# Top-k of the experts in four parts of two heads in place of two parts of four

## The chip, the cores and the metric

The program runs on 1 core of a Trainium2 chip. The metric is the device time of one execution in microseconds; before the change it was 2129.03 us, the median of 3 runs (2128.95 to 2151.08). Engines are PE (matrix), DVE (vector), ACT (scalar), POOL (GpSimd) and SP (which here only issues transfers); the core has 16 DMA engines.

## The reference

One layer on 512 prompt rows and 32 sample rows (8 sequences of 4). An attention block (compressed, selected and window keys) and a convolution are mixed and added to x; then each row looks up experts:

```
h2 = rms_norm(x, norm2) * (1 + sc2) + sh2
q  = (h2 @ peer_q).reshape(rows, 8 heads, 2, 128)
s  = einsum(q, peer_keys)                # 128 scores for each head and half
s1, i1 = top_k(s[half 0], 16);  s2, i2 = top_k(s[half 1], 16)
cand = s1[:, None] + s2[None, :]         # 256 candidates a head
top_s, pos = top_k(cand, 16)             # index of an expert = i1 * 128 + i2 at pos
g = softmax(top_s)                       # over the 16 of a head
a = gelu(h2 . u[expert]);  y = sum over 8 heads x 16 experts of (g * a) * v[expert]
x = x + gt2 * y
```

u and v of an expert lie side by side in one row of 8 KB. Everything is float32.

## The kernel before

**Tiles.** Rows are handled in 5 tiles: four of 128 prompt rows, and one for the 32 sample rows, which are spread so that each partition holds 2 of the 8 heads. A prompt tile needs 8 x 16 = 128 "columns" (one expert for each of the 128 rows), the sample tile 32: 544 columns in all, called rows n of the ring in the code and below. For column n POOL issues one indirect DMA (L1950) of 128 rows x 8 KB into slot n % 10 of the ring `expert_rows`; DVE takes the dot product with h2 (L1906); ACT makes gelu (L1386), weights (L1392) and a diagonal (L1402); PE adds the weighted v for two columns at a time into banks 0 to 3 (L1044) and with that frees two slots (`s_v`).

**Side work.** All else (the attention, the convolution, the queries and top-k of the next tile) is cut into slots and woven into the 544 columns in a fixed order on each engine. `make_plan` lists stages in windows; an item with two lanes runs them side by side, slot by slot. `SLOTS_OF` gives each stage its slots and a length. `slots_before` does the window before the first column as a whole, and says for each column how many slots stand before it; engines call `slots.upto(n)` in their loops, PE up to 4 columns ahead. All side work is placed before column 500, as the last 12 of the prompt columns are the time in which tile 4's first gathers must get their index.

**Queries and top-k.** The queries of a tile are 8 weight units (`pq` 0 to 7, 1 MB each, L848) in four quarters of two units and two heads; ACT copies each quarter from its bank (L1287). Stage query0 does units 0 to 3 and then the scores of two quarters (L870, one `keys` load of 512 KB for both), query1 the same for units 4 to 7. ACT copies scores (L1295). topk0 and topk1 (DVE, L1692 to L1758) each handle four heads: lists of 16 of the 128 scores (MAX8, FIND_INDEX8, MATCH_REPLACE8), a 1024-wide grid of sums, lists again, six 1024-wide operations that pick the index (L1744 to L1748), and a cast to `expert_index` (L1752), which adds one to `s_rt`. POOL waits for `s_rt` every 64 columns.

**Weights.** SP loads units in the order of the plan into a ring of 3 slots (`weight_units`); the load of unit j waits until unit j - 3 is used. `aside(key)` issues other transfers just before a given unit, so what it waits for holds up every later load. In front of ("in", 4, 5), the first glu unit of the sample tile, it loads x, waits for `s_rt`, and loads the convolution history (L2107) and the sample bias (L2110).

**Memory.** The scores of a tile lie in `stage_room` in two pieces of 1024 columns, and the lists of topk0 and topk1 in two areas (`Top16`).

## Time and profile before

| | |
|---|---|
| median of 3 runs | 2129.03 us |
| profiled execution, span from first to last instruction | 2124.2 us |
| PE / DVE / ACT / POOL busy | 75% / 58% / 37% / 33% |
| DMA moved | 782.11 MB, mean 368 GB/s |
| gathers (q0) / other transfers (q1), share of 16 engines | 65.1% / 25.9% |
| first gather issued / first column dotted | 254.74 us / 275.65 us |

The profile was taken of one execution; its own span stands 4.8 us below the median of the runs. A row of the profile's timeline gives start and length in us, engine, line, operation and operands; what stands in brackets is the time in which the engine was idle before, and what ended it. A DMA share of 1.00 is all 16 engines at work.

### The profile page before, as it was taken

To read this page: it belongs to the slowest core of one execution; us is meant where nothing else is said; L and a number is where in the kernel's file an instruction comes from. 1 tells how busy PE (TensorE), PEld (TensorE's weight loads), DVE (VectorE), ACT (ScalarE), POOL (GpSimd) and SP (SyncE) were. 2 spreads that over 40 slices of the span, in tenths; PEclk is the share of its full clock that TensorE was granted. 3 is DMA by queue.
4 is the path that set the end of the run, shared out by engine and by line. 5 is a ranking of instruction groups with operands and counts; after the bars stand their busy time and mean duration, and the time that the engine had idled before them with its cause. 6 is when DMAs were issued, how large, how long until landed. Compare 5 with 4: busy or idle time off the path is not lost.

```text
span 2124.2 us, 29781 instructions
## 1 busy us (share of the span) xinstructions
PE 1587.9 (75%) x10176; PEld 954.1 (45%) x10176; DVE 1232.5 (58%) x3327; ACT 781.4 (37%) x2217; POOL 701.2 (33%) x611
## 2 busy tenths in 40 slices
PE   6976658795967788758888685889687786759533
PEld 4845534443644445535534363556254342426200
DVE  0132566794586795488598459643555353443754
ACT  2132144384245375334367422352412132332322
POOL 0850112342323343223443322434323323323442
PEclk9786878687979699879888887969889868778765
DMA  7773899998999989899999998999989988999996
GB/s 270 244 288 109 328 376 426 422 364 366 375 394 426 421 369 396 353 426 378 424 426 359 393 398 351 426 378 396 425 321 389 384 329 320 375 419 370 417 417 284
DMA packets 149994, 782.11 MB, mean 368 GB/s; under 512 B 17392, under 2 KB 53136, under 8 KB 60932
## 3 DMA queue, kind: packets, MB, share of 16 engines
q0 software_dynamic: 78336, 570.46, 65.1%
q1 hardware_dynamic: 71509, 209.77, 25.9%
q8 instruction: 81, 1.33, 0.2%
q14 instruction: 68, 0.56, 0.1%
HBM read 773.75 MB, written 10.99 MB: 369 GB/s over the span
## 4 chain that ended last, share of the span: by engine, by line
PE 39%; DMA 24%; DVE 18%; issue 8%; ACT 7%; SPq 2%; POOL 1%; POOLq 0%; ACTq 0%; DVEq 0%
DMA expert_rows<-in_expert_uv,expert_index 16%; PE bank L1044 13%; DVE expert_rows L1906 6%; PE bank L921 5%; PE bank L848 5%; PE bank L728 3%; PE bank L667 3%; PE bank L832 3%; DMA gate_or_shift_and_scale<-mod_dram 2%; DVE conv_out L1518 2%; PE bank L639 2%; DMA weight_units<-in_w_ada_units 2%; DMA weight_units<-in_w_out_units 2%; POOL expert_rows L1950 1%; PE bank L999 1%
## 5 line engine op out<-in xcount | busy, mean ns | idle before, releaser
L1950 POOL DMA_INDIRECT expert_rows<-in_expert_uv,expert_index x544 | 629.3, 1157 | 1333.4 <-PE bank L1044 1086.4
L1906 DVE CUSTOM_DVE_ANT_0 expert_rows<-expert_rows,h_rows 128x1024 f32<-128x1024 f32 x544 | 658.8, 1222 | 384.7 <-DMA expert_rows<-in_expert_uv,expert_index 374.1
L1044 PE MATMUL bank<-expert_rows,weight_diagonals 64*64 64x512 f32 x4096 | 605.3, 716 | 104.3 <-ACT weight_diagonals L1402 83.5
L1386 ACT ACTIVATE group_gelu<-group_dots 128x2 f32<-128x2 f32 x272 | 55.5, 204 | 804.4 <-DVE group_dots L1906 790.6
L1044 PEld LDWEIGHTS bank<-expert_rows,weight_diagonals 64*64 64x64 f32 x4096 | 151.4, 153 | 364.8 <-issue 216.8
L848 PEld LDWEIGHTS bank<-stage_room,weight_units 128*128 128x128 f32 x1280 | 153.7, 200 | 37.6 <-issue 31.4
L1402 ACT ACTIVATE weight_diagonals<-consts_sb,group_weights 128x64 f32<-128x64 f32 (+1 forms) x544 | 158.8, 340 | 17.1 <-ACT group_weights L1392 0.7
L848 PE MATMUL bank<-stage_room,weight_units 128*128 128x128 f32 (+1 forms) x1280 | 161.2, 286 | 4.3 <-ACT stage_room L1275 3.5
L1392 ACT ACTIVATE group_weights<-group_gelu,expert_gate 128x1 f32<-128x1 f32 x544 | 131.3, 288 | 9.4
L921 PE MATMUL bank<-weight_units,prompt_bias 128*128 128x256 f32 x512 | 128.7, 401 | 0.0
L1518 DVE SCALAR_TENSOR_TENSOR conv_out<-stage_room,small_weights,conv_out 128x128 f32<-128x128 f32 (+1 forms) x480 | 125.1, 319 | 0.0
L921 PEld LDWEIGHTS bank<-weight_units,prompt_bias 128*128 128x128 f32 x512 | 97.3, 198 | 39.1 <-issue 27.0
L1386 ACT ACT_TABLE_LOAD x81 | 103.9, 1283 | 1.4
L728 PEld LDWEIGHTS bank<-compress_pairs,weight_units 128*128 128x128 f32 x512 | 85.0, 262 | 27.8 <-issue 27.8
L832 PE MATMUL bank<-weight_units,stage_room 128*128 128x256 f32 (+1 forms) x320 | 77.7, 401 | 22.7 <-DVE stage_room L1662 17.8
L667 PE MATMUL bank<-weight_units,stage_room 128*128 128x256 f32 (+1 forms) x400 | 92.6, 387 | 2.6 <-DMA weight_units<-in_w_in_units 2.6
L639 PEld LDWEIGHTS bank<-stage_room,weight_units 128*128 128x128 f32 x640 | 82.0, 211 | 27.7 <-issue 15.9
L639 PE MATMUL bank<-stage_room,weight_units 128*128 128x128 f32 (+1 forms) x640 | 85.5, 297 | 8.9 <-ACT stage_room L1109 8.9
L728 PE MATMUL bank<-compress_pairs,weight_units 128*128 128x16 f32 (+1 forms) x512 | 87.0, 321 | 0.0
L667 PEld LDWEIGHTS bank<-weight_units,stage_room 128*128 128x128 f32 (+1 forms) x400 | 68.8, 176 | 33.4 <-issue 17.0
L832 PEld LDWEIGHTS bank<-weight_units,stage_room 128*128 128x128 f32 (+1 forms) x320 | 57.0, 182 | 47.8 <-DVE stage_room L1662 21.9
L1047 PE MATMUL bank<-expert_rows,weight_diagonals 128*32 128x512 f32 x128 | 28.8, 1052 | 53.7 <-ACT weight_diagonals L1402 43.5
(250 smaller groups left out, 1648.2 us busy)
## 6 DMA issues: line engine op xcount, KB each, us to landing
weight_units<-in_w_in_units SPq DMA_DIRECT2D x45, 1024.0 KB
weight_units<-in_peer_q_units SPq DMA_DIRECT2D x40, 1024.0 KB
weight_units<-in_w_ada_units SPq DMA_DIRECT2D x24, 1024.0 KB
weight_units<-in_w_out_units SPq DMA_DIRECT2D x20, 1024.0 KB
weight_units<-in_w_units SPq DMA_DIRECT2D x16, 1024.0 KB
expert_rows<-in_expert_uv,expert_index POOLq DMA_INDIRECT x544
weight_units<-in_cmp_pages SPq DMA_DIRECT2D x128, 64.0 KB
gate_or_shift_and_scale<-mod_dram SPq DMA_DIRECT2D x12, 512.0 KB
```

The source lines that it names most:

```text
L639: last = mm(out[:, a * P:a * P + r], w[:, k, a * P:(a + 1) * P], hT(i, k), start=(k == 0), stop=(k == KD - 1))
L667: last = mm(out[0:r, c * 256:(c + 1) * 256], hT(i, k), w[:, k], start=(k == 0), stop=(k == KD - 1))
L728: last = mm(out[:, c:c + g3 * n].rearrange("p (g c) -> p g c", g=g3), w[:, s, hh * P:(hh + 1) * P], e.rT[:, kv, s, 0:g3, one + lo:one + hi ...
L832: last = mm(out[0:r, 0:256], e.catT[:, k, 0:r], w[:, k], start=(k == 0), stop=(k == KD - 1))
L848: last = mm(out[:, c:c + r], w[:, k, a * P:(a + 1) * P], e.h2T[:, k, 0:r], start=(k == 0), stop=(k == KD - 1))
L921: last = mm(dst, e.w1_s[:, one, s, hh * P:(hh + 1) * P], w[:, :, :, s], start=False, stop=(one == 1 and s == 7))
L1044: last = mm(e.bank[2 * a + c][o * HD:(o + 1) * HD, :], e.diag[ps, m % (NG * GR)], e.ring[ps, m % RING, cs], start=first, stop=final)
L1386: do(e.act_v[:, p], e.dots[:, p], ACT.Gelu_apprx_tanh).then_inc(e.s_gelu, 1)
L1402: do(e.diag[:, p * GR + j, 0:unit.shape[1]], unit, ACT.Copy, scale=e.wv[:, p, j:j + 1]).then_inc(e.s_d, 1)
L1518: ins = vec.scalar_tensor_tensor(out, src, w[:, ct, k:k + 1], out, ALU.mult, ALU.add)
L1906: vec.tensor_tensor_reduce(out=row, in0=row, in1=e.h2[:, i % 2], scale=1.0, scalar=0.0, op0=ALU.mult, op1=ALU.add, accum_out=e.dots[:, q % ...
L1950: pool.indirect_dma_start(e.ring[:, n % RING], None, e.io["expert_uv"], bass.IndirectOffsetOnAxis(ap=e.eidx[:, i % 2, j:j + 1], axis=0)).t ...
```

## The change

Scores, top-k, gate softmax and gathers go in parts of two heads, 32 columns each: `topk0` to `topk3`. There is one stage `query` in place of query0 and query1; the scores of quarter q are computed in the middle of the first unit of quarter q + 1, and `keys` are loaded in four pieces of 256 KB, each in a slot of its own. The room of the lists is one area used by all parts, which reaches over the convolution history's place, so SP's wait in front of that load is now for all parts of tile 3. The planner starts topk0 12 slots after `query` (in the window before the first column too, which now holds topk0 of two heads), puts a pad of 36 slots before x of tile 1, places the mixing of tiles 2 to 4 by a column and searches for the pace that ends all at column 500.

```diff
 class Top16:
-        self.half, self.half_i, self.half_f = lists(a[:, 0:128]), lists(a[:, 128:256], U32), lists(a[:, 256:384])
+        self.half, self.half_i, self.half_f = lists(a[:, 0:64]), lists(a[:, 64:128], U32), lists(a[:, 128:192])
...
-    e.scores = [room[:, a:a + 1024].rearrange("p (a n) -> p a n", a=PH) for a in (1024, 3072)]
-    e.top16 = [Top16(room[:, 4096:4864], room[:, 4864:4992]), Top16(room[:, 2304:3072], room[:, 4096:4224])]
+    e.scores = [room[:, a:a + 512].rearrange("p (a n) -> p a n", a=4) for a in (1024, 1536, 3072, 3584)]
+    e.top16 = Top16(room[:, 4096:4416], room[:, 5048:5176])
...
-            "conv": (43, 0), "cmp": (22, 11), "mix": (18, 10), "query0": (20, 11), "query1": (19, 12.5), "topk0": (31, 8),
-            "topk1": (31, 9), "sc": (42, 24), "satt": (90, 44)}
+            "conv": (43, 0), "cmp": (22, 11), "mix": (18, 10), "query": (37, 23.5), "topk": (20, 5), "sc": (42, 24), "satt": (90, 44)}
...
-    def chain(i, ahead):
-        return [[ahead + [("x", i), ("glu", i)], [("topk1", i - 1)]], ("z", i),
+    def chain(i, ahead, behind):
+        return [[ahead + [("x", i), ("glu", i)], behind], ("z", i),
                 [[("cmp", i), ("att", i)], [("conv", i)]],
-                ("mix", i), ("query0", i), [[("query1", i)], [("topk0", i)]]]
+                ("mix", i), [[("query", i)], [("gap", 12), ("topk0", i), ("topk1", i)]]]
+    def late(i):
+        return [("topk2", i), ("topk3", i)]
...
-                ("mix", 0), ("query0", 0), [[("query1", 0)], [("topk0", 0)]]]]
-    windows.append(chain(1, [("ada3", 0)]))
+                ("mix", 0), [[("query", 0)], [("gap", 12), ("topk0", 0)]]]]
+    windows.append(chain(1, [("ada3", 0), ("pad", 36)], [("topk1", 0)] + late(0)))
...
 def slots_before(windows):
+    room, low, high = FIRST[PT] - 12.0, 0.5, 2.0
+    for _ in range(40):
+        pace = (low + high) / 2
...
+                    if name == "mix" and i > 1:
+                        start = max(start, FIRST[i - 1] + 8.0)
+            ends += [start + pace * length_of(item) * (s + 1) / k for s in range(k)]
+        low, high = (pace, high) if ends[-1] < room else (low, pace)
...
+def query_units(i):
+    out = [("pq", i, u) for u in range(8)]
+    if i == PT:
+        return out + [("keys", i, q) for q in range(4)]
+    for q in range(3):
+        out.insert(3 * q + 3, ("keys", i, q))
+    return out + [("keys", i, 3)]
...
+        for u in range(8):
+            w, j = units.take(("pq", i, u)).rearrange("p (k n) -> p k n", k=KD), units.n - 1
+            q = u // 2
...
+                if a == 0:
+                    yield
+                    if u % 2 == 0 and q and i < PT:
+                        scores_of(i, q - 1, last_scores)
...
     def topk(i, part):
-        nh = 4 if i < PT else 2
+        nh = 2
...
-            if j % 64 == 0:
-                pool.wait_ge(e.s_rt, 2 * i + j // 64 + 1)
+            if j % 32 == 0:
+                pool.wait_ge(e.s_rt, 4 * i + j // 32 + 1)
...
-            sp.dma_start(slot[:, 0:D], io["keys_unit"][:, key[2] * D:(key[2] + 1) * D]).then_inc(sem, 16)
+            sp.dma_start(slot[:, 0:4 * P], io["keys_unit"][:, key[2] * 4 * P:(key[2] + 1) * 4 * P]).then_inc(sem, 16)
...
             if i == PT:
-                sp.wait_ge(e.s_rt, 2 * PT - 1)
+                sp.wait_ge(e.s_rt, 4 * PT)
                 sp.dma_start(e.cs, io["conv_history"]).then_inc(e.s_hist, 16)
```

Where the planner puts stages, in columns (the column before which the first and the last slot of a stage stand):

| stage | before | after |
|---|---|---|
| top-k of tile 0 that is left | 0 to 14 | 0 to 22 |
| x and glu of tile 1 | 3 to 13 | 15 to 23 |
| mixing of tiles 1, 2, 3, 4 | 61, 158, 264, 459 | 69, 165, 270, 462 |
| queries of tile 1 | 71 to 89 | 79 to 95 |
| queries of tile 3, then first pages of tile 4 | 274 to 292, 297 | 279 to 295, 303 |
| last top-k of tile 3 | 297 to 315 | 314 to 325 |
| glu of tile 4 | 324 to 333 | 329 to 338 |
| queries and top-k of tile 4 | 469 to 492, 492 to 499 | 472 to 495, 495 to 499 |

The order on PE at the end of the window before the first column and in the first columns. Before (L882 turns h2, L848 are queries, L870 scores, L608 and L600 the last modulation units, L624 turns x of tile 1, L639 its glu, L1044 columns):

```order
L882 MATMUL bank<-consts_sb,h_rows 128x128 x8
L848 MATMUL bank<-stage_room,weight_units 128x128 x64
L870 MATMUL bank<-weight_units,stage_room 128x128 x8
L848 MATMUL bank<-stage_room,weight_units 128x128 x64
L870 MATMUL bank<-weight_units,stage_room 128x128 x8
...
L600 MATMUL bank<-y_half_sums,consts_sb 9x256 x2
L624 MATMUL bank<-consts_sb,stage_room 128x128 x8
L1044 MATMUL bank<-expert_rows,weight_diagonals 64x512 x8
L639 MATMUL bank<-stage_room,weight_units 128x128 x16
```

After (L893 queries, L868 scores, L622 modulation, L1058 columns, L646 the turn of x, L661 glu):

```order
L878 MATMUL bank<-consts_sb,h_rows 128x128 x8
L893 MATMUL bank<-stage_room,weight_units 128x128 x40
L868 MATMUL bank<-weight_units,stage_room 128x128 x4
L893 MATMUL bank<-stage_room,weight_units 128x128 x32
L868 MATMUL bank<-weight_units,stage_room 128x128 x4
...
L622 MATMUL bank<-y_half_sums,consts_sb 9x256 x2
L1058 MATMUL bank<-expert_rows,weight_diagonals 64x512 x48
L646 MATMUL bank<-consts_sb,stage_room 128x128 x8
L1058 MATMUL bank<-expert_rows,weight_diagonals 64x512 x8
L661 MATMUL bank<-stage_room,weight_units 128x128 x20
```

The first scores stand behind 40 query matmuls and not 64, and twelve columns (six pairs) come before the turn of x of tile 1.

The order on SP of the loads of a prompt tile's queries. Before:

```order
L1975 DMA weight_units<-in_peer_q_units 128x2048 x2
L1977 DMA weight_units<-in_keys_unit 128x1024
L1975 DMA weight_units<-in_peer_q_units 128x2048 x4
L1977 DMA weight_units<-in_keys_unit 128x1024
```

After:

```order
L1981 DMA weight_units<-in_peer_q_units 128x2048
L1983 DMA weight_units<-in_keys_unit 128x512
L1981 DMA weight_units<-in_peer_q_units 128x2048 x2
L1983 DMA weight_units<-in_keys_unit 128x512
L1981 DMA weight_units<-in_peer_q_units 128x2048 x2
L1983 DMA weight_units<-in_keys_unit 128x512
L1981 DMA weight_units<-in_peer_q_units 128x2048
L1983 DMA weight_units<-in_keys_unit 128x512
```

Two more loads take a whole slot each of the ring of three.

## Rows read from the trace of the kernel before

**Rows 1.** The page, parts 1 and 3.

```profile
PE 1587.9 (75%) x10176; PEld 954.1 (45%) x10176; DVE 1232.5 (58%) x3327; ACT 781.4 (37%) x2217; POOL 701.2 (33%) x611
...
q0 software_dynamic: 78336, 570.46, 65.1%
q1 hardware_dynamic: 71509, 209.77, 25.9%
```

**Rows 2.** Windows of the run: busy time by engine, PEclk, DMA share, GB/s.

```profile
200.00:235.00 35.00, 29.85 (x243) 29.29 (x244) 11.13 (x65) 4.11 (x7) 0.00 (x0) 0.87 0.63 212
235.00:255.00 20.00, 11.63 (x124) 8.01 (x122) 19.28 (x54) 5.86 (x10) 0.26 (x1) 0.97 0.95 364
...
280.00:300.00 20.00, 10.43 (x68) 6.53 (x72) 17.14 (x66) 10.92 (x29) 1.93 (x2) 0.63 0.76 295
300.00:2000.00 1700.00, 1334.76 (x8520) 780.97 (x8509) 1065.80 (x2836) 674.22 (x1894) 568.85 (x492) 0.84 0.95 388
2000.00:2107.00 107.00, 45.20 (x248) 8.78 (x240) 61.00 (x98) 30.58 (x119) 48.92 (x40) 0.66 1.00 413
```

**Rows 3.** Waits of the POOL queue, summed: us, times, longest.

```profile
POOL expert_rows L1950 <- PE bank L1044: 1086.4, 234, 27.6
POOL expert_rows L1950 <- DVE expert_index L1752: 119.7, 1, 119.7
```

**Rows 4.** Timeline of DVE, first top-k: start, length, line, operands [idle before].

```profile
224.86 0.87 DVE L1707 MAX8 stage_room<-stage_room 128x8 f32<-128x128 f32 x4 [21.16 <-ACT stage_room L1295]
...
253.61 0.19 DVE L1752 CAST expert_index<-stage_room 128x64 int32<-128x64 f32 x1
...
275.65 1.23 DVE L1906 CUSTOM_DVE_ANT_0 expert_rows<-expert_rows,h_rows 128x1024 f32<-128x1024 f32 x1 [18.96 <-DMA expert_rows<-in_expert_uv,expert_index]
```

**Rows 5.** DVE groups by shape, and one 512-wide row of the last top-k.

```profile
L1746 DVE TENSOR_TENSOR stage_room<-stage_room 128x1024 f32<-128x1024 f32 x16 | 19.6, 1223 | 0.4
...
1993.07 0.69 DVE L1746 TENSOR_TENSOR stage_room<-stage_room 128x512 f32<-128x512 f32 x1
```

**Rows 6.** Timeline of PE in the prologue and at the first rows.

```profile
206.40 15.95 PE L848 MATMUL bank<-stage_room,weight_units 128*128 128x128 f32 x128 [0.68 <-ACT stage_room L1275]
223.07 2.02 PE L870 MATMUL bank<-weight_units,stage_room 128*128 128x128 f32 x16 [0.72 <-issue]
...
288.74 1.97 PE L624 MATMUL bank<-consts_sb,stage_room 128*128 128x128 f32 x8 [31.09 <-DVE stage_room L1469]
290.63 3.69 PE L1044 MATMUL bank<-expert_rows,weight_diagonals 64*64 64x512 f32 x16
```

**Rows 7.** Timeline of ACT: the copy of the first query quarter.

```profile
215.24 0.59 ACT L1287 COPY stage_room<-bank 128x512 f32<-128x512 f32 x1 [8.89 <-PE bank L848]
```

**Rows 8.** Timeline of POOL: the first gather and the first refill.

```profile
254.74 1.14 POOL L1950 DMA_INDIRECT expert_rows<-in_expert_uv,expert_index  x1 [119.70 <-DVE expert_index L1752]
...
294.63 0.96 POOL L1950 DMA_INDIRECT expert_rows<-in_expert_uv,expert_index  x1 [27.57 <-PE bank L1044]
```

**Rows 9.** Queries of the second prompt tile: SP's queue, then PE.

```profile
571.07 0.33 SPq L1977 DMA_DIRECT2D weight_units<-in_keys_unit  x1
...
574.54 1.95 PE L1044 MATMUL bank<-expert_rows,weight_diagonals 64*64 64x512 f32 x16
576.42 3.84 PE L848 MATMUL bank<-stage_room,weight_units 128*128 128x128 f32 x32
584.83 2.05 PE L870 MATMUL bank<-weight_units,stage_room 128*128 128x128 f32 x8 [4.57 <-issue]
```

**Rows 10.** The start of the sample tile: SP's queue, then PE, windows.

```profile
1324.71 0.41 SPq L2107 DMA_DIRECT2D stage_room<-in_conv_history  x1
...
1316.76 0.56 PE L917 MATMUL bank<-weight_units,prompt_bias 128*128 128x2 f32 x2 [18.52 <-issue]
...
1300.00:1320.00 20.00, 3.24 (x9) 2.73 (x10) 19.59 (x78) 4.52 (x18) 0.97 (x2) 0.54 0.89 345
```

**Rows 11.** Exponentials of the gates: the table load before each.

```profile
L1308 ACT ACT_TABLE_LOAD  x9: 1283/1283/1283, 242.8 to 1988.6; - x9
```

More of the change, by code:

```diff
@@ L403, in size_of @@
         return i, 0
+    if name == "pad":
+        return i, i / 4
+    if name.startswith("topk"):
+        return SLOTS_OF["topk"]
     if name == "att":
@@ L517, in weight_units @@
         "mix": lambda i: [("wo", i, q) for q in range(4)],
-        "query0": lambda i: [("pq", i, u) for u in range(4)] + ([("keys", i, 0)] if i < PT else []),
-        "query1": lambda i: [("pq", i, u) for u in range(4, 8)] + ([("keys", i, 0)] if i == PT else []) + [("keys", i, 1)],
+        "query": query_units,
         "sc": lambda part: [("pages", part // 2, part % 2 * 2 + s) for s in range(2)],
@@ new lines, in query @@
+        yield
+        if i < PT:
+            yield
+            scores_of(i, 3, prod.open(pe, ("scores", i, 3)))
+            return
+        prod.freed(pe, ("pq", i, 3))
+        out = prod.open(pe, ("scores", i, 0))
+        for q in range(4):
+            keys = key_part(i, q)
+            for a in range(4):
+                last = mm(out[q * NS:(q + 1) * NS, a * P:(a + 1) * P], e.q2T_s[:, 4 * q + a, 0:NS], keys[:, a],
+                          start=True, stop=True)
+            if q < 3:
+                units.used(last)
@@ L910, in sc @@
+        last.then_inc(prod.ready, 1)
+        units.used_by(("scores", i, 0))
     def sc(part):
@@ L1269, in mix, with query @@
         root(slice(36, 37), r, D).then_inc(e.s_x1q, 1)
-    def query0(i):
+    def query(i):
         r = rows(i)
@@ L1276, in query0, with kept @@
             last.then_inc(prod.free(("h2T", i, q)), 1)
-        yield
-        yield from query_half(i, 0)
-    def query_half(i, half):
-        r = rows(i)
-        for q in range(2 * half, 2 * half + 2):
-            for _ in range(8):
+        def kept(q):
+            out = prod.wait(act, ("scores", i, q))
+            nc.scalar.copy(e.scores[q].rearrange("p a n -> p (a n)"), out[:]).then_inc(prod.free(("scores", i, q)), 1)
+        for q in range(4):
+            for _ in range(3):
+                yield
+            if q and i < PT:
+                kept(q - 1)
+            for _ in range(6 if q == 0 else 5):
                 yield
@@ L1288, in query_half @@
                            ).then_inc(prod.free(("pq", i, q)), 1)
-        if i == PT and half == 0:
-            return
-        for q in range(2 if i < PT else 1):
-            key = ("scores", i, 2 * half + q if i < PT else 0)
-            out = prod.wait(act, key)
-            dst = e.scores[half if i < PT else 0][:, 4 * q:4 * q + 4]
-            nc.scalar.copy(dst.rearrange("p a n -> p (a n)"), out[:]).then_inc(prod.free(key), 1)
-            if q == 0:
-                yield
+        for _ in range(3):
+            yield
+        kept(3 if i < PT else 0)
     def topk(i, part):
-        n = 4 if i < PT else 2
-        for _ in range(21 if i < PT else 11):
+        for _ in range(11):
             yield
-        if i == PT and part:
-            return
-        j = 2 * i + part
+        j = 4 * i + part
         act.wait_ge(e.s_sx, j + 1)
-        g = e.gsm[:, i % 2, part * 64:part * 64 + n * TK]
+        g = e.gsm[:, i % 2, part * 32:part * 32 + 2 * TK]
         do(g, g, ACT.Exp).then_inc(e.s_gx, 1)
@@ L1724, in top16 @@
             yield
-        for a in range(nh // 2):
-            prod.freed(dve, ("scores", i, 2 * part + a))
-            yield from top16(scores, keep.half, keep.half_i, range(4 * a, 4 * a + 4))
+        prod.freed(dve, ("scores", i, part))
+        yield from top16(scores, keep.half, keep.half_i, range(4))
         pair = keep.half[:, 0:2 * nh].rearrange("p (h c) k -> p h c k", c=2)
@@ L1731, in topk @@
         yield
-        for a in range(nh // 2):
-            yield from top16(cand, keep.top, keep.top_i, range(2 * a, 2 * a + 2))
+        yield from top16(cand, keep.top, keep.top_i, range(2))
         top, top_i = keep.top[:, 0:nh], keep.top_i[:, 0:nh]
```

173 lines of the change are left out of this document (72 added, 101 removed).

## The prediction

> **What bounds the kernel now.** I read the page first. No engine is full: PE 75%, DVE 58%, ACT 37%, POOL 33%, while the two large DMA queues together hold the 16 DMA engines for 65.1 + 25.9 = 91% of the span [rows 1]. The windows say where. From 300 to 2000 us the DMA share is 0.95 at 388 GB/s, and from 2000 to 2107 it is 1.00; below that lie 200 to 235 us with 0.63 and 280 to 300 us with 0.76 [rows 2]. So once the expert gathers run, the kernel moves bytes nearly all the time. One gather is 128 rows of 8 KB, 1.05 MB, 2.5 us at the 413 GB/s of the last window, and there are 544 of them. This is the first thing to keep in mind: from the first gather on, the end moves only by DMA time that stands idle and is then used, or the other way round. Idle after 235 us is 0.05 x 20 = 1.0 us (235 to 255), 0.24 x 20 = 4.8 us (280 to 300) and 0.05 x 1700 = 85 us (300 to 2000).
>
> Then I read what POOL waited for. It waits once for an index, 119.7 us, before the very first gather; all its other large waits are for PE to give back a ring slot, 1086.4 us over 234 times [rows 3]. A gather is therefore late for want of an index only at the start. That finer top-k parts let tiles 1 to 4 issue earlier is worth nothing: their index is in time already.
>
> Last, the start itself. The first top-k begins at 224.86, its index is written at 253.61 and done at 253.80, the first gather issues at 254.74 and the first row is dotted at 275.65, 20.9 us after the issue [rows 4, 8]. PE, in order, has to run the turn L624 of the next tile's x before row 0; it waited 31.09 us for it, and the first pair of rows started at 290.63, the first refill at 294.63 [rows 6, 8]. Between, all ten slots had landed: that is the 4.8 us idle.
>
> **The change, part by part.**
>
> *Earlier first index.* PE's first query quarter is over when its copy starts, 215.24 [rows 7]. The score product of quarter 0 now stands behind half of the third unit: the 15.95 us are 128 entries for four units, so half a unit is 16 entries, 16 x 125 ns = 2.0 us; then comes half of the 2.02 us of L870, then a copy of 0.59 us [rows 6, 7]. With 0.3 us of hand-overs: 215.24 + 2.0 + 1.0 + 0.6 + 0.3 = 219.1 instead of 224.86. The first part has half the heads. Before it took 253.80 - 224.86 = 28.9 us for four; seven of its operations are 1024 wide and cost 1.223 us each, 8.6 in all, and 0.69 at 512, 4.8 in all [rows 4, 5]; the other 20.3 us are lists that halve to 10.2, and small operations that hardly do, 0.5 more: together some 15.5 us. Index at 234.6, first gather at about 235.5, which is 19.2 us earlier. The first row is then dotted at 235.5 + 20.9 = 256.4 if the same traffic stands before it.
>
> *x(1) and glu(1) leave the first rows.* The planner's pad of 36 slots puts them at rows 15 to 23; PE has six pairs of rows before L624 where it had none. The 31.09 us wait of L624 no longer stands before the first pair, so refills begin before the ring is full of landed rows.
>
> *What both are worth.* The traffic they meet is the same as before, only sooner: four ada units, x, the 4 MB copy of the window cache, three w_in units. Those kept the DMA engines at 0.95 from 235 to 255 already [rows 2]. So 19 us of earlier gathers buy only the idle: 1.0 + 4.8 = 5.8 us. Ends: 0, if a new pause opens when the three parts of top-k (15.5 us each) and 22 dots of 1.2 us make DVE the pace of rows 0 to 22, and 26 us, if the whole timeline moves with the first refill. I take **-6 us**, the side of the windows.
>
> *Queries, PE.* The matmuls are the same. What changes is the ring of three weight slots: a tile's queue was 8 units of 1 MB and 2 of keys, now 8 and 4 of a quarter MB, each in a whole slot. From pq3 on, a unit is often requested when only one other lies before PE, where it was two. In the prologue a unit of PE is about 4 us and hides most of a load; what is left delays the end of the queries by 1 or 2 us, in the shadow of the wait for the first gather. In tiles 1 to 3 a unit with a pair of rows is 3.84 + 1.95 = 5.8 us on PE [rows 9] and 3 MB, 7.5 us, on DMA: DMA is the longer. **0**; upper end below, with its rival.
>
> *DVE.* Four parts a tile instead of two. Two halves of a wide operation are 2 x 0.69 - 1.22 = 0.16 us more, seven of them 1.1 us, some nine small ones at about 0.19 us 1.7 us: 2.8 us for each of eight pairs of parts, 22 us of an engine that is 58% busy. **0**; uncovered 22 us.
>
> *ACT.* Gate exponentials go from 9 to 17; each pulls in one table of 1.283 us and gives the gelu table back, 2.6 us [rows 11]: 8 x 2.9 = 23 us, on the way from dot to diagonal, under DMA time. **0**; uncovered 23 us.
>
> *The sample tile's start.* PE stood 18.52 us at L917 for the first pages, in a window with share 0.89 [rows 10]. The plan leaves 8 rows between query and pages of tile 4, where it left 5; three rows are 9 us or so, and the idle there (0.11 x 20 = 2.2 us in that window alone) shrinks: **-3 us** (0 to -5). Against it: SP now waits for all four parts of tile 3, planned for row 325, before it loads the convolution history, which it issued at 1324.71, near row 302 [rows 10]. Queued behind are the sample bias and three w_in units, 4.5 MB, 11 us of transfers; PE needs the first at row 329. While SP stands, gathers have DMA alone, but PE was busy there. **+2 us** (0 to 11).
>
> *The last keys.* Four key units end the queue in a ring of three, so the last is only asked for when the first is used. A key load took from 571.07 to 584.83 to be used, 13.8 us [rows 9]. The last top-k then starts up to 5 us later with the ring's ten rows ahead of it: **+1 us** (0 to 10).
>
> *Sum*: -6 - 3 + 2 + 1 = -6, on a span of 2124.2: 2118. The median of the runs, 2129.0, lies 4.8 above that span; the same 4.8 gives **2123 us**. I have said nothing of the other 80 us idle between 300 and 2000. Every tile's stages now stand 3 to 8 rows later and denser, and each pause (mixing, a new tile's attention) can grow or shrink by a few us; with four tiles I allow 12 us to each side.
>
> The one rule that speaks against this: the Trainium skill, "DMA: Bandwidth & Descriptors", section "Anatomy of one DMA", gives every transfer a fixed 2.0 us beside its bytes and says that a transfer below some 860 KB is less than half efficient. Ten more key loads would by that be 20 us more if nothing ran beside them, an estimate of about 2143 in place of 2123. No row here shows a key load alone; the windows at 1.00, with two queues in flight, speak for the fixed part being hidden.
>
> **Rivals.**
> *A. The timeline moves with the start.* If rows after 300 us are paced by the row chain (dot, gelu, diagonal, matmul, refill) and not by bytes, the 19.2 us of the first gather come through whole, and up to 26 with the first refill: 2129 less 19 to 26, about **2106**. For it: POOL waits on PE 234 times. Against: DMA share 0.95 while it does.
> *B. Weights come late (slower).* Place: the queries of tiles 1 to 3, pq3 to pq7. A load asked for one unit ahead has 5.8 us; the only measured contended one was 13.8 us, so 8 us missing, five times a tile, 40 us. PE works in order, so rows wait with it, but ten rows in the ring keep DMA busy for 25 us; what is over, 15 us, counts three times: 2123 + 45 = **2168**. It decides from the point where 5 x (load - 5.8) exceeds 25, a load of 10.8 us. For it: 13.8 is above that. Against: that load shared the queue with x and a large unit, and a load gets quicker as the gathers before it run out.
> *C. Nothing moves.* The first gather is early but waits in the queue for the copy of the window cache, the new places of the pauses cancel the rest: **2129**.
>
> **Chances.** About 1%, 21 us, is what I call a change: below 2108 faster, above 2150 slower. Forecast 0.52 (0.03 of it faster, 0.03 slower), A 0.20 (0.17 faster), B 0.14 (0.12 slower), C 0.14. That is faster 0.20, same 0.65, slower 0.15. The forecast's own range is 2106 to 2142 (12 us of pauses and the ends of the small terms). To hold 8 in 10 the range goes down over A, to 2098, and up towards B, to 2150.
>
> **What the new profile would show.** First gather near 235.5 and first dot near 256: the first part is right. Share 0.95 or more from 235 to 310: the 6 us; if there is a pause near 300 to 330 with DVE full, DVE paced the first rows. POOL's wait for an index once only. Share of 300 to 2000 still near 0.95: the bound is bytes; the gain is then the difference in idle, not 19 us. In the queries of tiles 1 to 3, PE waits for units of a few us with share 1.0; if share falls there, B. SP's history load near row 325, and PE's first glu of the sample tile waiting under 10 us. I am wrong if the idle of 300 to 2000 changes by more than 15 us, either way, or if the start takes or gives something that the windows do not show.

## The result

The changed kernel takes 2152.74 us (median of 4 runs, 2151.83 to 2159.26) beside 2134.82 us of the kernel before (4 runs): ratio 1.0097, 95% interval [1.0056, 1.0139]. Two more comparisons of the same two kernels on other chips gave 1.0145 [1.0071, 1.0218] and 1.0083 [1.0044, 1.0121]; the three, weighted by their intervals, give 1.0097 +/- 0.0026, 21 us. The forecast was 2123.0, with 2150 as the upper end. A ratio is always of runs that share their chip, and it is not the quotient of the two medians (here 1.0084); medians of different chips are not compared. Runs more than 1.5% above the fastest of the same kernel are left out of the ratios (in a_thrice 3 of 12).

The profiled execution has a span of 2150.0 us. Its page, parts 1 and 3, answers to [rows 1]:

```profile
PE 1594.2 (74%) x10176; PEld 956.8 (45%) x10176; DVE 1250.5 (58%) x3463; ACT 795.8 (37%) x2236; POOL 698.8 (33%) x611
...
q0 software_dynamic: 78336, 570.46, 65.0%
q1 hardware_dynamic: 72949, 209.77, 25.5%
```

The bytes are the same. The packets of both queues took 90.5% of 2150.0 = 1945.8 us, before 91.0% of 2124.2 = 1933.0. So of the 25.8 us of span, about half (13.0) is time in which the DMA engines stood idle and half (12.8) time in which they took longer over the same bytes. Windows and POOL's waits, answering to [rows 2, 3]:

```profile
200.00:235.00 35.00, 28.13 (x214) 27.16 (x215) 16.68 (x63) 5.03 (x8) 0.00 (x0) 0.83 0.51 177
235.00:255.00 20.00, 11.48 (x91) 10.46 (x93) 2.14 (x10) 2.34 (x4) 9.60 (x10) 0.87 0.98 374
280.00:300.00 20.00, 12.43 (x60) 2.64 (x52) 18.84 (x63) 6.50 (x18) 6.32 (x6) 0.50 0.92 365
300.00:340.00 40.00, 18.20 (x104) 8.53 (x99) 32.95 (x112) 17.30 (x44) 9.49 (x8) 0.69 0.82 327
300.00:2000.00 1700.00, 1319.11 (x8467) 778.48 (x8461) 1072.00 (x2935) 687.41 (x1909) 561.72 (x484) 0.84 0.95 384
```

```profile
POOL expert_rows L1956 <- PE bank L1058: 1122.0, 225, 33.3
POOL expert_rows L1956 <- DVE expert_index L1758: 102.4, 1, 102.4
```

From 300 to 2000 us the share is 0.95 as before but moves 384 GB/s and not 388: over 1700 us that is 4 x 1.7 = 6.8 MB, some 18 us at that rate (both rates are rounded). The pause at 280 has shrunk (0.76 to 0.92), and a new one stands behind it: 300 to 340 has 0.82 at 327 GB/s, where the same window of before has:

```profile
300.00:340.00 40.00, 32.16 (x228) 21.50 (x218) 29.33 (x65) 19.18 (x40) 12.44 (x12) 0.91 1.01 425
```

**The start.** DVE answers to [rows 4], then PE in the first columns:

```profile
220.35 0.87 DVE L1715 MAX8 stage_room<-stage_room 128x8 f32<-128x128 f32 x4 [15.74 <-ACT stage_room L1294]
235.79 0.18 DVE L1758 CAST expert_index<-stage_room 128x32 int32<-128x32 f32 x1
263.28 0.41 DVE L1466 TENSOR_TENSOR y_rows<-bank,gate_rows 9x256 f32<-9x256 f32 x1 [26.01 <-PE bank L622]
264.67 1.19 DVE L1912 CUSTOM_DVE_ANT_0 expert_rows<-expert_rows,h_rows 128x1024 f32<-128x1024 f32 x1
```

```profile
307.15 3.69 PE L1058 MATMUL bank<-expert_rows,weight_diagonals 64*64 64x512 f32 x16 [6.29 <-ACT weight_diagonals L1412]
316.94 3.69 PE L1058 MATMUL bank<-expert_rows,weight_diagonals 64*64 64x512 f32 x16 [6.10 <-ACT weight_diagonals L1412]
330.04 1.97 PE L646 MATMUL bank<-consts_sb,stage_room 128*128 128x128 f32 x8 [9.41 <-DVE stage_room L1479]
331.94 3.45 PE L1058 MATMUL bank<-expert_rows,weight_diagonals 64*64 64x512 f32 x16
```

The index is written at 235.97, the first gather issues at 236.91 (POOL). But the first dot, at 264.67, shows no wait for its expert row: DVE, in order, stood 26.01 us at L1466 for the first product of the last modulation units (L622 on PE). Later, pairs come 9.8 and 15.0 us apart, PE waiting for diagonals and for x(1) (L646), while DVE is busy 32.95 of 40 us.

**The queries.** PE's waits for query weights, summed (us, times, longest): after, where L893 are the queries and L917 the sample tile's scores, and before (the one such wait; 2.3 us in b_again, a second profile of the kernel before):

```profile
PE bank L893 <- DMA weight_units<-in_peer_q_units: 27.6, 16, 3.6
PE bank L917 <- DMA weight_units<-in_keys_unit: 5.4, 1, 5.4
```

```profile
PE bank L848 <- DMA weight_units<-in_peer_q_units: 0.6, 1, 0.6
```

**The sample tile.** SP's queue after (x, history, glu units and the pages behind them) and PE's two waits at the products with pages (L931), then the same pages before and PE's second such wait there (L917; the first is in [rows 10]):

```profile
1357.43 0.37 SPq L2023 DMA_DIRECT2D x_rows<-in_x_sample  x1
1408.35 0.35 SPq L2113 DMA_DIRECT2D stage_room<-in_conv_history  x1
1409.22 16.09 SPq L1975 DMA_DIRECT2D weight_units<-in_w_in_units  x4
1439.70 37.52 SPq L1987 DMA_DIRECT2D weight_units<-in_cmp_pages  x32
...
1347.12 0.56 PE L931 MATMUL bank<-weight_units,prompt_bias 128*128 128x2 f32 x2 [13.07 <-issue]
1467.60 0.56 PE L931 MATMUL bank<-weight_units,prompt_bias 128*128 128x2 f32 x2 [9.79 <-issue]
```

```profile
1411.17 35.69 SPq L1981 DMA_DIRECT2D weight_units<-in_cmp_pages  x32
1433.34 0.56 PE L917 MATMUL bank<-weight_units,prompt_bias 128*128 128x2 f32 x2 [4.41 <-issue]
```

SP stands 50.6 us between x and history. PE's wait for the first pages is 5.5 us shorter, its wait for the next pages 5.4 us longer. The rows put these waits down to "issue"; that they are waits for pages is read from SP's queue, and in a_thrice one of them (13.86 us) is named as such.

**Where the time goes, by bytes.** From the records of all packets one can read when the first N MB had landed. Below: how many us each stretch of bytes took more than in the kernel before. The marks are, in columns of before, 35, 155, 210, 273, 333, 397 and the end. The first row is a second profile of the kernel before. Between profiles of one kernel a stretch mostly differs by up to 5 us, but from 440 to 520 MB the three of the changed kernel give 3, 4 and 14.

```
MB moved                  0-120 -280 -360 -440 -520 -600 -781 | sum
kernel before, again        2    -3    0   -1   -1   -1   -4  |  -8
changed                     7    -8   10    6    3   -1   10  |  25
changed, again              6    -8   12    1    4    1   11  |  26
changed, third              6    -5   11    3   14    0    7  |  37
a_keys_own_again            7   -13    5    0    8    1   10  |  17
a_scores_late_again         6    -9    6    3    0   -1    7  |  12
a_keys_history_again        4   -14    3    1    1    1    3  |  -2
a_start_two                 2   -11    5    3   -1   -3    7  |   0
b_keys_four                 8    -3   -5    1    0    5    7  |  13
a_late_four                 9    -6    6    3   12   -1    7  |  32
a_late_four_history         9    -2    9    3    7    1   10  |  37
a_scores_late_history       5    -8   11    3    4    1    7  |  23
a_flat                      6    -8   14   -7   19    1   10  |  35
a_pad14                    15    -2   10    7    9    4   -3  |  40
```

A profile is one execution: b_keys_four sums to 13 while its 12 timed runs are level with before. The table says where, the ratios say how much.

### The profile page after: what moved, and what is told of

The parts are those of the page before. It is cut to its first block, busy times and chain, and to the rows that moved or that the text cites. A ratio compares the mean times of both kernels' runs of the same rounds, so it can differ in the third digit from the quotient of the medians.

```text
span 2150.0 us, 29982 instructions
## 1 busy us (share of the span) xinstructions
PE 1594.2 (74%) x10176; PEld 956.8 (45%) x10176; DVE 1250.5 (58%) x3463; ACT 795.8 (37%) x2236; POOL 698.8 (33%) x611
## 3 DMA queue, kind: packets, MB, share of 16 engines
q0 software_dynamic: 78336, 570.46, 65.0%
## 4 chain that ended last, share of the span: by engine, by line
PE 44%; DMA 24%; DVE 14%; issue 8%; ACT 6%; SPq 2%; POOL 1%; another core or an unknown queue 1%; POOLq 0%; ACTq 0%; DVEq 0%
PE bank L1058 13%; DMA expert_rows<-in_expert_uv,expert_index 11%; PE bank L935 6%; DVE expert_rows L1912 5%; PE bank L893 5%; PE bank L854 4%; DMA weight_units<-in_peer_q_units 3%; PE bank L689 3%; DMA weight_units<-in_w_ada_units 2%; PE bank L750 2%; PE bank L661 2%; DMA gate_or_shift_and_scale<-mod_dram 2%; PE bank L813 2%; DMA weight_units<-in_win_keys 1%; POOL expert_rows L1956 1%
## 5 line engine op out<-in xcount | busy, mean ns | idle before, releaser
L1058 PE MATMUL bank<-expert_rows,weight_diagonals 64*64 64x512 f32 x4096 | 606.3, 718 | 95.9 <-ACT weight_diagonals L1412 83.0
L1058 PEld LDWEIGHTS bank<-expert_rows,weight_diagonals 64*64 64x64 f32 x4096 | 153.3, 154 | 366.2 <-issue 223.0
L893 PE MATMUL bank<-stage_room,weight_units 128*128 128x128 f32 (+1 forms) x1280 | 167.9, 290 | 29.7 <-DMA weight_units<-in_peer_q_units 27.6
L893 PEld LDWEIGHTS bank<-stage_room,weight_units 128*128 128x128 f32 x1280 | 158.1, 203 | 62.8 <-DMA weight_units<-in_peer_q_units 32.8
L661 PEld LDWEIGHTS bank<-stage_room,weight_units 128*128 128x128 f32 x640 | 79.7, 207 | 19.8 <-issue 15.9
L661 PE MATMUL bank<-stage_room,weight_units 128*128 128x128 f32 (+1 forms) x640 | 82.4, 291 | 3.5 <-ACT stage_room L1123 2.1
L750 PEld LDWEIGHTS bank<-compress_pairs,weight_units 128*128 128x128 f32 x512 | 75.0, 235 | 21.9 <-issue 21.9
L750 PE MATMUL bank<-compress_pairs,weight_units 128*128 128x16 f32 (+1 forms) x512 | 76.8, 300 | 0.0
```

What stands on the lines that cost most here:

```text
L661: last = mm(out[:, a * P:a * P + r], w[:, k, a * P:(a + 1) * P], hT(i, k), start=(k == 0), stop=(k == KD - 1))
L750: last = mm(out[:, c:c + g3 * n].rearrange("p (g c) -> p g c", g=g3), w[:, s, hh * P:(hh + 1) * P], e.rT[:, kv, s, 0:g3, one + lo:one + hi ...
L893: last = mm(out[:, c:c + r], w[:, k, a * P:(a + 1) * P], e.h2T[:, k, 0:r], start=(k == 0), stop=(k == KD - 1))
L1058: last = mm(e.bank[2 * a + c][o * HD:(o + 1) * HD, :], e.diag[ps, m % (NG * GR)], e.ring[ps, m % RING, cs], start=first, stop=final)
```

## The experiments

**The changed kernel again** (a_again, a_thrice), and **the kernel before again** (b_again), unaltered.

> The changed kernel once more, unaltered, for a second trace and times beside the kernel before on the same chip. If its excess is its own, the ratio to the kernel before lies between 1.005 and 1.014 again, and the same pauses of the DMA engines stand at columns 259, 281 and 345. If part of the excess belongs to the single execution (the packets of the gathers took 342 ns in its last 50 us and 309 ns in the kernel before), the packet times differ in this trace while the pauses stay.

> The changed kernel once more, as the run to compare the next ones with on the same chip. Both theories: ratio to the kernel before 1.009 to 1.014.

> The kernel before once more, for a second trace. Of the 25 us between the spans of the two first traces 11 are idle DMA time and 14 are packets that took longer for the same bytes. If the second part belongs to the program, this trace shows a busy time of the DMA engines near that of the kernel before (some 1937 us); if it is chance, it may lie up to 14 us higher. Ratio 0.997 to 1.003.

Ratios 1.0145, 1.0083 and 1.0004 [0.997, 1.0038]. PE's waits for query weights were again 27.4 us in a_again and 27.0 in a_thrice. The loss is the program's own.

**Keys outside the ring** (a_keys_own). The four key parts of a prompt tile go into 512 free columns of the stage room, with a semaphore of their own.

```diff
-    for q in range(3):
-        out.insert(3 * q + 3, ("keys", i, q))
-    return out + [("keys", i, 3)]
+    return out
...
+        sp.dma_start(e.keybuf, io["keys_unit"][:, q * 4 * P:(q + 1) * 4 * P]).then_inc(e.s_kl, 16)
```

> The changed kernel, but the key parts of the prompt tiles go to a free piece of stage_room and no longer take slots of the ring of three weight units. Theory 1 (key loads in ring slots make the query units late): the waits of PE for peer_q units, 27.6 us in all in the changed kernel, fall below 5 us, the prologue's idle DMA time falls by 3 to 4 us, and the time by 8 to 12 us, to a ratio of 1.003 to 1.006. Theory 2 (the places of the stages, above all attention of tile 3 lying over the handover of the banks at column 256): the waits fall too, but the time by less than 3 us.

> The changed kernel with the keys outside the ring, again, on the same chip as the next two, so that the history's part is read side by side. Measured before: ratio 1.0052 to the kernel before. Both theories: 1.004 to 1.007, 2141 to 2146.

Ratios 1.0052 [1.0016, 1.0088] and 1.0034 [0.9999, 1.007]: together 1.0043, which is 0.0054 +/- 0.0037 or 11 us (4 to 19) under the changed kernel, with as many DMAs and as many key bytes. PE's waits fall, to 5.5 us in a_keys_own and in a_keys_own_again to:

```profile
PE bank L892 <- DMA weight_units<-in_peer_q_units: 4.8, 4, 1.9
```

It also shows what held the first dot. SP's modulation loads, in the changed kernel and in a_keys_own:

```profile
241.39 15.48 SPq L1973 DMA_DIRECT2D weight_units<-in_w_ada_units  x4
```

```profile
234.12 11.01 SPq L1974 DMA_DIRECT2D weight_units<-in_w_ada_units  x4
...
250.61 1.19 DVE L1913 CUSTOM_DVE_ANT_0 expert_rows<-expert_rows,h_rows 128x1024 f32<-128x1024 f32 x1
```

In the prologue the key slots put the first modulation unit back by 7 us and the end of the four issues by 12 (245.1 to 256.9), and with them the first dot, which DVE reaches only behind L1466, from 250.6 to 264.7.

**Units, keys and scores in the old order** (a_scores_late): two key loads of 512 KB, scores of two quarters after the fourth and the eighth unit; top-k stays in four parts.

```diff
-        out.insert(3 * q + 3, ("keys", i, q))
-    return out + [("keys", i, 3)]
+    return out[0:4] + [("keyh", i, 0)] + out[4:8] + [("keyh", i, 1)]
...
-                ("mix", i), [[("query", i)], [("gap", 12), ("topk0", i), ("topk1", i)]]]
+                ("mix", i), [[("query", i)], [("gap", 19), ("topk0", i), ("topk1", i)]]]
```

> The changed kernel with the units, keys and scores of the queries as in the kernel before (four units, keys of two quarters, scores of both), top-k still in four parts; top-k of each tile starts 7 slots later. Theory 1: PE's waits for peer_q fall below 5 us, and the time by 8 to 12 us although the first index is some 6 us later. Theory 2: within 4 us of the changed kernel. Theory 3 (the early first index is worth its full 19 us and something else costs more): the first gather 6 us later makes it 6 us slower than the changed kernel.

> The changed kernel with units, keys (two of 512 KB) and scores in the order of the kernel before, again: ratio 1.002 to 1.005 by both theories.

1.0036 [0.9999, 1.0072] and 1.0053 [1.0018, 1.0088], query waits 5.7 and 6.2 us. Together that is 1.0045, 11 us (3 to 19) under the changed kernel. By another way it gives back as much as a_keys_own: this half of the loss lies in the key slots and not in finer top-k, which both keep. The other half is still there in both.

**Four key slots alone in the kernel before** (b_keys_four).

```diff
-        "query0": lambda i: [("pq", i, u) for u in range(4)] + ([("keys", i, 0)] if i < PT else []),
+        "query0": lambda i: [("pq", i, u) for u in range(4)] + ([("keys", i, 0), ("keys", i, 1)] if i < PT else []),
```

> The kernel before with one part of the change: the keys of a prompt tile are four loads of 256 KB, each in a slot of the weight ring, in place of two of 512 KB; scores, top-k and plan stay. After a quarter of the queries two small units now end the line, so the weight unit behind them is asked for with less work ahead of PE. Theory 'ring' (the slots cost about 10 us of the changed kernel's 18 to 25): PE's waits for query weights rise from 0.6 us to 10 or more, idle DMA time at equal bytes rises by 2 to 4 us, time 5 to 10 us over the kernel before, about 2139. It is a weaker dose than in the changed kernel, where the small units stand between the large ones. Rival 'placement' (key slots hurt only where scores stand inside the units and the rest of the plan is changed too): within 2 us of the kernel before, 2132.

Ratio 0.9992 [0.996, 1.0023], and yet:

```profile
PE bank L848 <- DMA weight_units<-in_peer_q_units: 18.1, 5, 5.9
```

"Ring", as I had put it, fell here: PE waits 18 us more and the end does not move. By bytes 8 us are lost before column 35 and made up by 360 MB.

**The same slots in the changed plan** (a_late_four): a_scores_late with two key units of 256 KB where it had one of 512.

```diff
-    return out[0:4] + [("keyh", i, 0)] + out[4:8] + [("keyh", i, 1)]
+    return out[0:4] + [("keys", i, 0), ("keys", i, 1)] + out[4:8] + [("keys", i, 2), ("keys", i, 3)]
```

> As the run ahead, but with four key loads of 256 KB, two behind the fourth and two behind the last query unit, each in a slot of the ring; scores still by halves of a tile's queries. Theory 'place' (the slots between the query units cut the look-ahead inside a running queue of units, and scores inside a unit hold the next release back; slots at the end of a half do no harm, as in the kernel before with four key slots): ratio within 0.002 of the run ahead, 1.002 to 1.006, with PE waiting some 15 us for query weights. Theory 'number' (in the changed plan any wait for weights comes through, however the slots lie): 1.008 to 1.012, as the changed kernel.

Ratio 1.0169 [1.0119, 1.022], 26 us (14 to 38) above a_scores_late, slower even than the changed kernel, with nearly the waits of b_keys_four:

```profile
PE bank L889 <- DMA weight_units<-in_peer_q_units: 20.0, 5, 6.3
```

"Place" fell; "number" has the direction, but its 1.008 to 1.012 lies below the measured interval. One edit costs 0 in one plan and 26 us in the other. In bytes, a_late_four loses 9 us to column 35 as b_keys_four does; at 360 MB b_keys_four is level again and a_late_four 9 us behind. It loses 12 more from 440 to 520 MB, at tile 3's last queries and the sample tile's start, the stretch in which profiles of one kernel differ most.

**SP's wait for the history.** a_history puts the lists of parts 2 and 3 elsewhere, so that SP waits for part 1 only; the same edit on a_keys_own (where SP also waits for the last scores), a_late_four and a_scores_late.

```diff
-    e.top16 = Top16(room[:, 4096:4416], room[:, 5048:5176])
+    e.top16 = [Top16(room[:, 4096:4416], room[:, 5048:5176]), Top16(room[:, 2304:2624], room[:, 2624:2752])]
...
-                sp.wait_ge(e.s_rt, 4 * PT)
+                sp.wait_ge(e.s_rt, 4 * PT - 2)
```

> The changed kernel, with the lists of parts 2 and 3 in the place of the turned queries, so that SP's wait before the convolution history is for the first two parts of tile 3 and not for all four. In the changed kernel SP stood 51 us there and PE waited 9.8 us for pages at the next compression part, with pauses of DMA at columns 309 and 345. Theory 4 (this wait is the other part of the loss): the history load is issued some 40 us earlier, that wait of PE falls under 5 us, and the time falls by 5 to 9 us. Against it (the forecast's 2 us): less than 3 us.

> Both repairs on the changed kernel: keys outside the ring of weight units, and the earlier history load. If the two losses are separate they add: 8 to 12 and 5 to 9 us less than the changed kernel, which is the kernel before or up to 5 us better (ratio 0.997 to 1.001). If they share one cause (SP late in general) the sum is no more than 12 us and the ratio 1.004 or more.

> Keys outside the ring and the convolution history loaded after half of the last top-k, again. If the history's wait is worth 8 us once the queries no longer starve, the ratio to the run beside it is 0.996 or less: 2134 beside 2142. Rival (the 8 us came of two different chips): 3 us or less between the two.

> a_late_four (four key slots at the ends of the halves, scores by halves) with the lists of parts 2 and 3 elsewhere in the stage room and SP waiting for part 1 only before the convolution history. Theory 'the history's wait turns late queries into lost time': the 12 us between 440 and 520 MB go, ratio 1.008 to 1.011 against 1.0169 without this edit. Rival 'the key slots delay PE by themselves': the 12 us stay, ratio 1.014 to 1.019.

> a_scores_late with the same edit on the history: the control. Theory: there are no late queries to turn into a loss, so 0 to 3 us less than without the edit, ratio 1.002 to 1.005. Rival: as much is gained as in the run ahead, ratio under 1.000, and the wait's price does not hang on the key slots.

```
                without           with the edit
changed         1.0097            1.0103 [1.0044, 1.0163]
a_keys_own      1.0043            1.0021 [0.9995, 1.0046], 1.0025 [0.999, 1.0059]
a_late_four     1.0169            1.0113 [1.0072, 1.0154]
a_scores_late   1.0045            1.0022 [0.9993, 1.0051]
```

Three of the four fall, by 4, 12 and 5 us, but each interval reaches over zero (12 +/- 14 for the largest), and on the changed kernel nothing shows, though the history was issued at 1356.10 in place of 1408.35: PE's wait for the next pages, which I expected to fall under 5 us, was 13.7. All four together give 5 +/- 5 us. Side by side on one chip, a_keys_history_again lies 2 us under a_keys_own_again by their ratios (9 by their medians). The wait may be worth some 5 us, which is not shown, and I can't say that it is what turns late queries into lost time: a_late_four_history is still 19 us (0.0091 +/- 0.005) over its control.

**The pause at the hand-over to tile 2 of the prompt** (a_flat): no side work in the five columns from 128, 256 and 384.

```diff
+    for first in FIRST[1:PT]:
+        for j in range(first, first + 5):
+            before[j] = before[first - 1]
```

> The changed kernel with one rule more in the planner: the five columns from each of 128, 256 and 384 on carry no side work (their slots stand behind them), so that PE's and DVE's handover of the banks isn't stretched by attention between. Theory 2: the pause at column 259 (15.3 us of idle DMA in the changed kernel, 20.9 us in which POOL issues nothing) shrinks to 8 us or less, and the time falls by 6 to 10 us. Theory 1: the pause shrinks, but is made good elsewhere or only moved; the time stays within 3 us.

Ratio 1.0089 [1.0056, 1.0123] beside 1.0097: unchanged. Windows of the changed kernel, then of a_flat:

```profile
1160.00:1190.00 30.00, 24.59 (x114) 15.19 (x109) 18.68 (x50) 14.99 (x35) 3.76 (x4) 0.60 0.49 195
1280.00:1320.00 40.00, 30.44 (x250) 22.11 (x251) 35.97 (x128) 10.27 (x30) 9.92 (x9) 1.00 0.99 392
```

```profile
1160.00:1190.00 30.00, 24.27 (x135) 14.56 (x136) 22.70 (x64) 14.34 (x41) 6.93 (x6) 0.83 1.01 416
1280.00:1320.00 40.00, 31.80 (x248) 23.02 (x252) 35.48 (x119) 9.78 (x28) 10.01 (x8) 0.96 0.90 349
```

The largest pause of the profile (share 0.49) is cured, and part of it comes back 120 us later (0.99 to 0.90). The bytes show the rest: from 360 to 440 MB a_flat is 13 us faster than the changed kernel, and from 440 to 520 MB 16 us slower (one profile each). A pause that is seen is not yet time that can be had.

**The start.** a_pad14 puts x(1) back near its old columns; a_start_two, on top of a_keys_history, puts tile 0's second top-k part back before the first column; a_start_two_pad14 does both.

```diff
-    windows.append(chain(1, [("ada3", 0), ("pad", 36)], [("topk1", 0)] + late(0)))
+    windows.append(chain(1, [("ada3", 0), ("pad", 14)], [("topk1", 0)] + late(0)))
```

```diff
-                ("mix", 0), [[("query", 0)], [("gap", 12), ("topk0", 0)]]]]
-    windows.append(chain(1, [("ada3", 0), ("pad", 36)], [("topk1", 0)] + late(0)))
+                ("mix", 0), [[("query", 0)], [("gap", 12), ("topk0", 0), ("topk1", 0)]]]]
+    windows.append(chain(1, [("ada3", 0), ("pad", 36)], late(0)))
```

> The changed kernel with a pad of 14 slots in place of 36: x and glu of tile 1 start near column 8 and not 15, and every later stage of tile 1 stands some columns earlier. Theory 3 (with the pad, DVE's three top-k parts alone pace columns 5 to 20 and DMA idles; 8 us were lost between 80 and 120 MB): the loss there shrinks to under 4 us, and the time falls by 3 to 6 us. If it is only the places of all later stages that matter, the early part improves and the time doesn't.

> The kernel with the keys outside the ring and the earlier history, and with the second part of tile 0's top-k moved back before the first column, as it stood before the change; the first index is still that of two heads, and the pad of 36 slots stays. Theory 'DVE paces the first columns': with 15.5 us of top-k less beside the first twenty columns the pauses near 290 and 330 us shrink, idle DMA time by 120 MB falls by 4 to 8 us, and the end comes 3 to 6 us earlier, about 2130, under the kernel before. The second part fits in the 20 us in which the first gather is under way, so the first dot moves by less than 2 us. Rival 'it is ACT or the order of PE': the pauses stay and the time is that of the run without this edit within 2 us, 2134. A second rival: the first dot slips by the 15.5 us and the time goes up by 5 or more.

> Keys outside the ring, earlier history, second part of tile 0's top-k before the first column, and now also the pad of 14 slots in place of 36, so that x and glu of tile 1 stand near their old columns. If the pad's only use was to let DVE do top-k beside the first columns, it is not needed any more: idle DMA time by 120 MB falls under 88 us and the time to 2128 or less, ratio 0.996 to 0.999. Rival (as with the pad of 14 in the changed kernel alone: the turn of x stands before the first pairs and refills wait): ratio 1.002 to 1.005.

a_pad14: 1.0139 [1.0094, 1.0184], not better; its first 120 MB come 15 us later than before, where the pad of 36 has 7. a_start_two: 0.9996 [0.9968, 1.0024], its first dot at 253.76 and its stretch to 120 MB 2 us over before where a_keys_history_again has 4. Beside that kernel (1.0022) it is 6 us less with an interval over zero (and 1 us more by the medians of the chip that they share); beside a_keys_own 10 us less (2 to 18). The pause that it was to cure is still there, though DVE is busy 26.85 of these 40 us, less than the 29.33 of the kernel before, which has no pause:

```profile
300.00:340.00 40.00, 24.30 (x151) 12.18 (x144) 26.85 (x69) 20.52 (x49) 12.63 (x10) 0.62 0.85 338
```

So a full DVE is not what makes it. An untested rival is the granted clock: in these 40 us it is 0.62 to 0.69, before 0.91, and a pair takes PE 3.69 us there, 1.95 elsewhere. With the pad of 14: 1.0021 [0.999, 1.0051]. So the best that I found of this change is level with the kernel before; no run beat it.

## Why the prediction was wrong

**The step that failed** is "Queries, PE ... 0": I costed the key slots' shorter look-ahead at nothing because DMA is the longer side of a unit. Removing the slots in two ways gave back 11 us each. The mechanism was rival B's, weights that come late, the size not: not waits of 8 us five times a tile, but 16 of at most 3.6 us, 27.6 us in all, and a loss of 11 us in place of 45. B's test (a load of over 10.8 us) was the wrong one: there is a loss though no single wait comes near 8 us. PE at the second prompt tile, answering to [rows 9]:

```profile
575.47 3.84 PE L893 MATMUL bank<-stage_room,weight_units 128*128 128x128 f32 x32 [3.02 <-DMA weight_units<-in_peer_q_units]
583.51 1.16 PE L868 MATMUL bank<-weight_units,stage_room 128*128 128x128 f32 x8 [0.35 <-DMA weight_units<-in_keys_unit]
588.54 1.16 PE L893 MATMUL bank<-stage_room,weight_units 128*128 128x128 f32 x8 [2.09 <-DMA weight_units<-in_peer_q_units]
```

That ten slots of the expert ring cover such waits was what I held against rival B, and b_keys_four says that it is a good reason in the kernel before. It does not hold in the changed plan (a_late_four). Which property of that plan takes the cover away is **open**; what the runs exclude is the mid-unit place of scores and keys, and the history's wait as the whole of it. Forecast and result lie 27 us apart (-6 and +21). The slots are 11 of these and the 6 us of the next term more. The other 10 are those that a_keys_own keeps over the kernel before and a_start_two doesn't; its two edits, to the history's wait and to tile 0's top-k, aren't clear of noise one by one.

**Earlier first index, -6.** Index at 235.97 for 234.6, first gather 236.91 for 235.5: right. First dot 256 forecast, 264.67 measured: I took over the 20.9 us from gather to dot and didn't look at what stands before the dot on DVE, the modulation operation L1466. In the kernel before its counterpart also stands ahead of the first dot, but had run 20 us earlier:

```profile
255.22 0.41 DVE L1456 TENSOR_TENSOR y_rows<-bank,gate_rows 9x256 f32<-9x256 f32 x1
```

The key slots put that operation back; without them the dot is at 250.6, 15.8 us after the first gather of a_keys_own (234.85) and without a wait. The pause "near 300 to 330 with DVE full" came, but a_start_two has it with DVE at 26.85 of 40 us, so my reading of that sign was wrong; and the six pairs ahead of x(1) did not keep refills going. At 120 MB the changed kernel is 7 us behind, at 280 level: the term came out as 0, not -6. Without the key slots some of it is there at 280 MB (a_keys_own_again 6 us ahead, a_start_two 9, one profile each) and is lost again later. Of rival A nothing showed, though the dot came 11 us sooner.

**DVE and ACT, 0.** DVE is busy 18.0 us more (22 reckoned), ACT 14.4 (23 reckoned; eight times the 2.6 us of the same sentence are 21). The gate tables are 17 as reckoned, but the gelu table is not given back each time, as the forecast had it: the loads at gelu's line go only from 81 to 83. Eleven more table loads of 1.283 us are 14.1 us, all of ACT's rise:

```profile
L1317 ACT ACT_TABLE_LOAD x17 | 21.8, 1283 | 0.3
L1396 ACT ACT_TABLE_LOAD x83 | 106.5, 1283 | 2.0 <-DVE group_dots L1912 0.5
```

a_scores_late keeps all of that and costs 10 us (0.0045 +/- 0.0025) over the kernel before, which bounds these two terms together with the new places; a_start_two keeps it too and is level.

**First pages, -3.** PE waits 5.5 us less there, and 5.4 more at the next pages [rows 10]; the two together are 22.9 us before and after, and 29.7 in a_again: nothing gained. **Wait for history, +2.** SP stood 50.6 us, but PE's first glu behind it (L661 at 1419.15) waited 1.02 us; removing the wait gave 4 and 5 us where the queries were well fed, neither clear of zero and both within the 0 to 11 that I had allowed. **Last keys, +1.** PE waited 5.4 us at L917, as said; every variant of the changed kernel keeps these four slots, so no run shows what they cost at the end.

**Pauses, +/-12, and the bound.** Idle grew by 13.0 us over the whole span, and from 300 to 2000 us, where 15 us were my sign of being wrong, the share stayed at 0.95. The sign did not show, and I was wrong all the same: I let the end move only by idle time. The same 780.2 MB of the two queues kept the engines 12.8 us longer, 15.4 and 19.2 in a_again and a_thrice, and 0.9 in a_start_two; a window's share of 0.95 hides that, its GB/s tell it. (The page rounds each share to 0.1%, 2 us of span.)

The Trainium skill, "DMA: Bandwidth & Descriptors", section "Anatomy of one DMA", whose fixed 2.0 us I weighed as 20 us for ten more loads, is by its heading about the SWDGE path, transfers that GpSimd issues; the key loads are SP's, so I had stretched it. Stretched so, it points the right way here by luck, for a reason that the runs contradict: b_keys_four has eight of these loads more (by that rule 16 us, an estimate) and its interval ends at +5 us, and a_keys_own keeps all ten and is 11 us faster. What is paid is the slot, not the transfer.

## What to carry to other kernels

In a short ring, count slots and not bytes: a small load that takes a whole slot takes a unit of look-ahead from the large ones behind it, and every load later in the same queue is put back with it. Before costing a wait at nothing because a deeper buffer covers it, ask whether that buffer is full when the wait comes, under the new plan and not the old; the same edit was free in one and 26 us in the other. And when a first result is made earlier, read what its consumer must do first in its own order.

## What I had not expected of the hardware

The same bytes in the same number of gathers took the DMA engines 12.8 to 19.2 us more of busy time in the three profiles of the changed kernel (1945.8, 1948.4, 1952.2) than in the two of the kernel before (1933.0, 1929.6), and 1933.9 in a_start_two with the changed kernel's packet counts. b_keys_four has 1153 packets more than the kernel before and 1933.1. So it is not the number of packets. By the shares of the page the whole excess is in the gathers: q0 took 1382.9 us before and 1397.5 after for the same 78336 packets (1400.0 in a_again, 1403.1 in a_thrice), while q1, with 1440 packets more, went from 550.2 to 548.3. What makes the gathers' packets longer was not isolated.
